# Scan sums from stacked high and low rows, transposes ahead of the state's products, and a later query transpose

## The chip, the cores and the metric

One core of a Trainium2 chip runs the whole program in one launch. The metric is the device time in microseconds (us); a profiled execution has a time of its own and a span, from its first to its last instruction. The kernel drives five instruction queues by hand: TensorE (PE: matmuls and transposes), VectorE (DVE), ScalarE (ACT), GpSimd (POOL) and SyncE (SP, which issues most DMAs). They meet only at semaphores.

## The reference, cut to what matters

Two layers. Each has three token mixers on one normalised input (a Mamba-2 scan, a gMLP, a dilated attention), an output projection and a gated FFN. The change touches the scan and the attention's queries. In the scan, for each chunk of 128 tokens, each of 2 directions and each of 8 heads (2 groups of 4), a 128x128 matrix of decays is needed:

```python
acs = jnp.cumsum((dt * a_neg).reshape(b, nc, q, g, hg), axis=2)
seg = acs[:, :, :, None] - acs[:, :, None, :]
decay_in = jnp.exp(jnp.where(tri[:, :, None, None], seg, NEG_INF))
cb = jnp.einsum('bctgn,bcsgn->bctsg', cc, bc)
y_diag = jnp.einsum('bctsg,bctsgh,bcsghp->bctghp', cb, decay_in, xdt)
states = jnp.einsum('bcsgn,bcsgh,bcsghp->bcghpn', bc, decay_out, xdt)
```

`y_off` adds what the state of the chunks before gives; the state goes from chunk to chunk in order.

## The kernel before, in words

All large products are float32 split in a high and a low part (fp32r), three matmuls per tile: weights high with input high, high with low, low with high. GpSimd makes the two parts of each weight unit (L475, L477) in two slots; PE frees a slot with its unit's first matmul of the next one (`w_used`).

**Layer, in the order of PE's queue.** Keys, queries, values (8 token tiles each), the 16 products `f` of the scan's input (`columns_tile`, 24 matmuls of 512 columns each, banks 0 and 1 in turn), attention with the gate's products between its steps, the backward states (`ra_`), the forward scan (`chunk`), the transposes of the mixers' outputs (`y_turn`), the output projection, the FFN.

**Keys and queries.** `heads_turn(f)`, f = 0 to 3, transposes 8 tiles of the normalised keys (f = 0, 1) or queries (2, 3) to PSUM banks 6 and 7. ACT takes the high part (`heads_high`, L1038) and DVE the low part (`heads_low`, L1446). `heads_turn(3)` waits until DVE has read banks 6 and 7 for f = 2, and that `heads_low(2)` waits for the copies KX<-KL by DMA (`keys_low`), since QL lies where KL lay. PE's queue has `heads_turn(3)` ahead of product f = 1. ACT's queue has `heads_high(3)`, two DMA issues (`queries_twice`), then `tap(0)` (it takes the products f = 0 and 1 from banks 0 and 1), `softplus`, `tap(1)` (products 2 and 3). Product f needs its bank emptied of product f - 2.

**Sums.** For chunk c, direction d and group g, bank 2 or 3 gets, for 4 heads, the sum of a mask (FAR: 0 or -1e30, by the identity IDR) and of the head's row of cumulated sums. Those rows lie transposed in the parameter tile `w_dt`, 128 rows: (chunk, direction, head). MH holds them in four copies, each with the rows of one head of the four and zeros elsewhere, ML the low parts. A stationary column of SEL, broadcast, picks the 4 rows of (c, d, g). So each of the four `sums` of a chunk is three matmuls of 512 columns: FAR, MH, ML (L803, L808). ACT takes the exponential (L1232).

**One chunk n in PE's queue** (`chunk`): the products of the states with C (L825, 8 instructions); sums j = 2 and 3; the gMLP's mix (L833) into bank 7; the state's products (L843) into the same bank 7, which first wait until DVE has read the mix (`gt_done`, GT, L1676); the next chunk's 6 transposes and 2 products B, C (`chunk_turn`, L792, L795); sums 0 and 1 of the next chunk; the 8 products within the chunk (L859), which wait for DVE's masked decays (`w_masked`, L1689).

**One chunk in DVE's queue** (L1669 to L1704): XW, CURF by its decay, Y1 from bank 5, GT from bank 7, Y3, YT's gMLP columns, twice the pair SEG add and SEG mask, CURF plus bank 7, Y1 three times, YT. **In ACT's:** XS from bank 0, BC from bank 1 (after the second mask), 8 exponentials, ST scaled, 8 more, Y2, the squares of the chunk before.

**Backward states** (`ra_`): PE's transposes (L743) and state products (L754); DVE XWA, BW; ACT BSTA, and at i = 2 IDR, SEL, MH; DVE at i = 4 `far` (FAR, ML). SP's queue reloads scan tiles (XBS, XBR) between two weight DMAs and the gates' loads.

Of the kernel before, what the change touches and what calls it, by code (L numbers as in the profile page):

```python
# [19 lines left out]
F32 = mybir.dt.float32  # L20
# [5 lines left out]
P = 128  # L26
# [107 lines left out]
def trunk(nc, xT, wst, params, consts, onehot, lnrow, table, outT):  # L134
# [10 lines left out]
    with ExitStack() as ctx:  # L145
# [12 lines left out]
        WH = place("WH", [P, W_AT[1] + 2048], dt=F32R)  # L158
        WL = place("WL", [P, W_AT[1] + 2048], dt=F32R)
        PARM = place("PARM", [P, NPAR])  # L160
        CST = place("CST", [P, 4 * P + 36])
        QSL = place("QSL", [P, AH_, P], top[0], F32R)
        U = place("U", [P, NT, 16])
        LDT = place("LDT", [P, NT, 16])
# [23 lines left out]
        NACS = place("NACS", [P, NT, 16])  # L188
        QGN = place("QGN", [P, 1])
        ident, tri_f, tri_b, ones = (CST[:, i * P:(i + 1) * P] for i in range(4))  # L190
        fourth, fours = CST[:, 4 * P:4 * P + 4], CST[:, 4 * P + 4:4 * P + 36]

        def par_(name, a=0, b=None):
            at, w = PAR[name]
# [70 lines left out]
        Y2 = work("Y2", [P, INNER])  # L265
        Y3 = work("Y3", [P, INNER])
        GT = work("GT", [P, GW])
        MH = place("MH", [P, 4, P], m_at[0], F32R)
        ML = place("ML", [P, 4, P], m_at[0] + 2048, F32R)
        IDR = place("IDR", [P, P], m_at[0] + 4096, F32R)  # L270
        FAR = place("FAR", [P, 2, P], m_at[0] + 4608, F32R)
        SEL = place("SEL", [P, 32], m_at[0] + 5632, F32R)
        assert m_at[0] + 5760 <= x_at

        PS = ctx.enter_context(nc.psum_tensor("PS", [P, 8, HALF], F32))

        def sem(name):
            return ctx.enter_context(nc.semaphore(name))
# [25 lines left out]
        xbs_used, zg_used = sem("xbs_used"), sem("zg_used")  # L304
        ra_t_full, ra_bst, ra_xw, ra_s_full, ra_done, ra_step = (
            sem("ra_t_full"), sem("ra_bst"), sem("ra_xw"), sem("ra_s_full"), sem("ra_done"), sem("ra_step"))
        acst_full, far_step = sem("acst_full"), sem("far_step")
        t_full, bst_ready, xs_ready = sem("t_full"), sem("bst_ready"), sem("xs_ready")
        ab_full, curf_ready, y12_done, gt_done = sem("ab_full"), sem("curf_ready"), sem("y12_done"), sem("gt_done")
        far_ready, ldt_ready = sem("far_ready"), sem("ldt_ready")  # L310
# [170 lines left out]
        def _(pe):  # L481
# [122 lines left out]
            for l in range(DEPTH):  # L604
# [47 lines left out]
                    pe.wait_ge(acs_ready, l + 1)  # L652
                    nc.tensor.transpose(PS[:, 4, 0:P], ACS[:].rearrange("p c e -> p (c e)"), ident).then_inc(acst_full, 1)

                between = {1: lambda: heads_turn(3), 6: decays, 8: decays_turn}
                for f in range(2 * XBC_T):
                    if f in between:
                        between[f]()
# [88 lines left out]
                def ra_state(i, par, first=False):  # L747
# [8 lines left out]
                                                XWA[:, par, g * 256:(g + 1) * 256], start=True, stop=True)  # L756
                    last.then_inc(ra_s_full, 1)

                def tile_in(i):
                    pe.wait_ge(xbs_full[i % 4], 16 * (l * (6 if i % 4 < 2 else 2) + i // 4 + 1))  # L760

# [8 lines left out]
                tile_in(1)  # L770
                ra_turn(1, 1)
                fold_head(STEPS - 1)
                ra_state(0, 0, first=True)
                pe.wait_ge(ra_t_full, l * NT + 2)
                pe.sem_inc(xbs_used, 1)
# [23 lines left out]
                def sums(n, j):  # L799

                        g, d = divmod(j, 2)
                        pe.wait_ge(exp_ready, n * 4 + j + 1)
                        nc.tensor.matmul(bank(2 + j % 2), IDR[:, :],  # L803
                                         FAR[:, d, :].unsqueeze(1).to_broadcast((P, 4, P)),
                                         start=True, stop=False, skip_group_check=True)
                        rows = n % NT * 4 + d * 2 + g
                        for part in (MH, ML):
                            last = nc.tensor.matmul(bank(2 + j % 2), SEL[:, rows:rows + 1].to_broadcast((P, P)),  # L808
                                                    part[:].rearrange("p h n -> p (h n)"), start=False,
                                                    stop=part is ML, skip_group_check=True)  # L810
                        last.then_inc(ab_full, 1)

                def chunk(i2, par, end):
                    c = i2 * 2 + par
                    n = l * NT + c

                    pe.wait_ge(curf_ready, 1 + n)
                    pe.wait_ge(y12_done, 1 + n)
                    if n:
                        pe.wait_ge(y2_ready, n)  # L820
                    for d in range(2):
                        for g in range(GROUPS):
                            cols = slice(g * 256, (g + 1) * 256)
                            st = CURF[:, cols] if d == 0 else BW[:, c + 1, cols]
                            last = nc.tensor.matmul(PS[:, 5 + d, cols], XBS[:, par, 6 + g, :], st,  # L825
                                                    start=True, stop=True)
                    last.then_inc(yo_full, 1)
                    sums(n, 2)
                    sums(n, 3)

                    pe.wait_ge(vn_ready, n + 1)
                    for g in range(GG):
                        last = nc.tensor.matmul(PS[:, 7, g * HD:(g + 1) * HD], par_("w_s", g * P, (g + 1) * P),  # L833
                                                ST[:, c // 4, c % 4, g * HD:(g + 1) * HD], start=True, stop=True)
                    last.then_inc(mx_full, 1)
                    pe.wait_ge(yo_full, n + 1)
                    pe.sem_inc(xbs_used, 1)

                    pe.wait_ge(bst_ready, n + 1)
                    pe.wait_ge(xw_ready, n + 1)  # L840
                    pe.wait_ge(gt_done, n + 1)
                    for g in range(GROUPS):
                        last = nc.tensor.matmul(PS[:, 7, g * 256:(g + 1) * 256], BC[:, 0, g, :],  # L843
                                                XW[:, g * 256:(g + 1) * 256], start=True, stop=True)
                    last.then_inc(sf_full, 1)
                    if not end:
                        pe.wait_ge(xbs_full[1 - par], 16 * (l * 6 + 2 + i2 + par + 1))
                        pe.wait_ge(bst_ready, n + 1)
                        chunk_turn(i2, 1 - par)
                        sums(n + 1, 0)  # L850
                        sums(n + 1, 1)

                    pe.wait_ge(xs_ready, n + 1)
                    pe.wait_ge(chunk_done, 1 + n)
                    for g in range(GROUPS):
                        pe.wait_ge(w_masked, 2 + n * 2 + g + 1)
                        for h in range(4):
                            e = g * 4 + h
                            last = nc.tensor.matmul(PS[:, 4, e * HD:(e + 1) * HD], SEG[par][:, 2 * g, h, :],  # L859
                                                    XS[:, par, e * HD:(e + 1) * HD], start=True, stop=True)  # L860
                    last.then_inc(yd_full, 1)
# [73 lines left out]
        def _(act):  # L935
# [85 lines left out]
            for l in range(DEPTH):  # L1021
# [84 lines left out]
                keys_low()  # L1106
                heads_high(2)
                act.wait_ge(row_out, 16)
                heads_high(3)
                queries_twice()  # L1110
                tap(0)
                softplus()
                tap(1)
                silu_out(0)
# [66 lines left out]
                for i in range(NT):  # L1181
                    n, par = l * NT + i, i % 2
                    act.wait_ge(ra_t_full, n + 1)
                    A(BSTA[:, par, :], PS[:, 1 + 3 * par, 0:GROUPS * STATE], ACT.Copy).then_inc(ra_bst, 1)
                    if i == 0:
                        gate(7)
                    if i == 2:
                        A(IDR[:], ident, ACT.Copy)
                        A(SEL[:], fours, ACT.Copy)
                        for h in range(4):  # L1190
                            last = A(MH[:, h, :], par_("w_dt"), ACT.Copy, scale=fourth[:, h:h + 1])
                        last.then_inc(far_step, 1)
                    if 1 <= i <= 4:
                        for t in range(2):
                            gate_square(2 * i - 2 + t)
                    if i == 6:
                        act.wait_ge(vinv_ready, l + 1)
                        A(VR[:], VSS[:], ACT.Sqrt).then_inc(vr_ready, 1)
# [19 lines left out]
                for c in range(NT):  # L1218
# [2 lines left out]
                    act.wait_ge(yz_ready, n + 1)  # L1221
                    A(XS[:, par], bank(0), ACT.Copy).then_inc(xs_ready, 1)
                    act.wait_ge(w_masked, 2 + n * 2)
                    A(BC[:].rearrange("p a g n -> p (a g n)"), bank(1), ACT.Copy).then_inc(bst_ready, 1)
                    for j in range(4):
                        g, d = divmod(j, 2)
# [74 lines left out]
        def _(dve):  # L1301
# [110 lines left out]
            for l in range(DEPTH):  # L1412
# [201 lines left out]
                def far():  # L1614
                    for d, tri in enumerate((tri_f, tri_b)):
                        TS(FAR[:, d, :], tri, 1.0, 1e30, ALU.subtract, ALU.mult)
                    dve.wait_ge(far_step, l + 1)
                    for h in range(4):
                        last = STT(ML[:, h, :], par_("w_dt"), fourth[:, h:h + 1], MH[:, h, :].bitcast(F32),
                                   ALU.mult, ALU.subtract)  # L1620
                    last.then_inc(far_ready, 1)

                step = Steps(dve, ra_step, 1)
# [218 lines left out]
def chip_constants():  # L1842
    i = np.arange(P)
    return np.concatenate([np.eye(P), i[:, None] <= i[None, :], i[:, None] >= i[None, :], np.ones((P, P)),
                           i[:, None] % 4 == np.arange(4), i[:, None] // 4 == np.arange(32)], axis=1).astype(np.float32)


def weight_stream(w_in, w_out, w_up, w_down):
# [73 lines left out]
```

## Time and profile before

| | |
|---|---|
| median of 3 runs | 2700.49 us (2696.34 to 2701.76) |
| profiled execution: time, span | 2702.63 us, 2700.8 us |
| busy: PE, DVE, ACT, POOL | 96%, 55%, 33%, 27% |
| mean granted TensorE clock | 0.986 |
| scan of layer 1, of layer 2 | some 436 to 520 us, 1764 to 1848 us |
| query stall of layer 1, of layer 2 | 123.5 to 129.2 us, 1452.0 to 1457.6 us |

Busy times of PE overlap by the end of one matmul and the start of the next; the distance from start to start is what a matmul costs in a full queue.

### The profile page before, as it was taken

How to read it: one execution, taken by the hardware profiler on the slowest of the kernel's cores; microseconds unless marked ns; L12 is line 12 of the kernel's file. 1: busy time of each engine (PE TensorE's matmuls, PEld its weight loads, DVE VectorE, ACT ScalarE, POOL GpSimd, SP SyncE). 2: the span in 40 equal slices, each digit the busy share in tenths (PEclk: the TensorE clock that was granted, in tenths of full speed). 3: DMA queues.
4: the chain of work that ended last, by engine and by line, in shares of the span. 5: the costliest groups of instructions: out<-in, count | busy, mean ns of one | idle time of the engine just before them, and what ended most of it. 6: DMA issues, size and time to landing. Idle time of an engine off the chain costs nothing.

```text
span 2700.8 us, 33553 instructions
## 1 busy us (share of the span) xinstructions
PE 2588.5 (96%) x13398; PEld 2188.8 (81%) x13398; DVE 1483.8 (55%) x1743; ACT 896.6 (33%) x1550; POOL 731.1 (27%) x388
## 2 busy tenths in 40 slices
PE   5999998899999999999999999898999999999998
PEld 5888987788888888888788889877878888888887
DVE  5466557837444444444564755686464444444455
ACT  3245556613222111111233465574131122211121
POOL 2332110023333333333323311200333333333331
PEclk9999999899999999999999999998999999999999
DMA  5434343121111111111122344521111111111111
GB/s 185 135 108 125 128 151 114 46 94 47 47 47 47 47 49 51 49 47 47 60 102 73 115 128 138 171 89 69 47 48 47 47 47 47 47 47 47 49 53 70
DMA packets 73724, 209.90 MB, mean 78 GB/s; under 512 B 5832, under 2 KB 28360, under 8 KB 72264
## 3 DMA queue, kind: packets, MB, share of 16 engines
q1 hardware_dynamic: 53384, 178.59, 20.0%
q10 hardware_dynamic: 20200, 29.30, 3.4%
q8 instruction: 106, 1.74, 0.3%
q14 instruction: 34, 0.28, 0.0%
HBM read 176.37 MB, written 31.49 MB: 77 GB/s over the span
## 4 chain that ended last, share of the span: by engine, by line
PE 87%; DVE 6%; ACT 3%; issue 2%; DMA 1%; POOL 0%; ACTq 0%; SPq 0%; DVEq 0%; POOLq 0%; PEldq 0%
PE PS L485 22%; PE PS L489 22%; PE PS L488 21%; PE PS L556 3%; PE PS L560 3%; PE PS L559 3%; PE PS L696 2%; PE PS L685 2%; DVE ACC L1311 1%; PE PS L808 1%; PE PS L825 1%; PE PS L859 1%; PE PS L675 1%; PE PS L674 1%; DVE CV L1484 1%
## 5 line engine op out<-in xcount | busy, mean ns | idle before, releaser
L485 PE MATMUL PS<-HH,WH 128*128 128x512 f32 x1920 | 760.2, 396 | 4.8 <-issue 4.8
L489 PE MATMUL PS<-HH,WL 128*128 128x512 f32 x1920 | 757.7, 395 | 0.0
L475 POOL CAST WH<-RAW 128x1024 fp32r<-128x1024 f32 x192 | 238.8, 1244 | 1910.7 <-PE PS L485 1430.3
L488 PE MATMUL PS<-HL,WH 128*128 128x512 f32 x1920 | 753.5, 392 | 0.0
L477 POOL TENSOR_TENSOR WL<-RAW,WH 128x1024 fp32r<-128x1024 f32 x192 | 498.0, 2594 | 15.4
L1740 DVE TENSOR_TENSOR X<-PS,X 128x512 f32<-128x512 f32 x384 | 259.3, 689 | 378.5 <-PE PS L489 378.0
L485 PEld LDWEIGHTS PS<-HH,WH 128*128 128x128 f32 x1920 | 363.0, 189 | 84.3 <-issue 5.6
L489 PEld LDWEIGHTS PS<-HH,WL 128*128 128x128 f32 x1920 | 362.4, 189 | 83.8
L488 PEld LDWEIGHTS PS<-HL,WH 128*128 128x128 f32 x1920 | 362.8, 189 | 82.1
L1270 ACT ACTIVATE FPAD<-PS 128x512 f32<-128x512 f32 x176 | 102.5, 596 | 890.5 <-PE PS L489 890.5
L1758 DVE SCALAR_TENSOR_TENSOR CVV<-FPAD,PARM,CVV 128x1024 f32<-128x1024 f32 x44 | 95.3, 2166 | 380.0 <-ACT CVV L1276 380.0
L485 PE MATMUL PS<-AHI,WH 128*128 128x512 f32 x704 | 277.4, 394 | 4.8 <-DVE X L1740 4.8
L489 PE MATMUL PS<-AHI,WL 128*128 128x512 f32 x704 | 278.5, 396 | 0.0
L488 PE MATMUL PS<-ALO,WH 128*128 128x512 f32 x704 | 276.5, 393 | 0.0
L556 PE MATMUL PS<-WH,HH 128*128 128x256 f32 (+1 forms) x896 | 262.1, 293 | 14.1 <-DVE HL L1332 14.1
L560 PE MATMUL PS<-WH,HL 128*128 128x256 f32 (+1 forms) x896 | 254.9, 284 | 0.0
L559 PE MATMUL PS<-WL,HH 128*128 128x256 f32 (+1 forms) x896 | 254.8, 284 | 0.0
L556 PEld LDWEIGHTS PS<-WH,HH 128*128 128x128 f32 x896 | 171.9, 192 | 17.1 <-DVE HL L1332 10.4
L560 PEld LDWEIGHTS PS<-WH,HL 128*128 128x128 f32 x896 | 172.4, 192 | 0.0
L559 PEld LDWEIGHTS PS<-WL,HH 128*128 128x128 f32 x896 | 171.7, 192 | 0.1
L485 PEld LDWEIGHTS PS<-AHI,WH 128*128 128x128 f32 x704 | 132.3, 188 | 36.5 <-DVE X L1740 6.6
L488 PEld LDWEIGHTS PS<-ALO,WH 128*128 128x128 f32 x704 | 132.3, 188 | 31.7
(198 smaller groups left out, 3122.6 us busy)
## 6 DMA issues: line engine op xcount, KB each, us to landing
RAW<-wst SPq DMA_DIRECT2D x192, 512.0 KB, 3.5
TOE<-toe_d SPq DMA_DIRECT2D x64, 512.0 KB, 3.7
XBS<-xbc_d SPq DMA_DIRECT2D x24, 512.0 KB, 4.4
xspill<-X ACTq DMA_DIRECT2D x2, 4096.0 KB, 12.3
xbc_d<-CV ACTq DMA_DIRECT2D x16, 512.0 KB, 4.5
X<-xspill SPq DMA_DIRECT2D x4, 2048.0 KB, 7.3
tok_d<-ST ACTq DMA_DIRECT2D x12, 512.0 KB, 3.4
ZG<-tok_d SPq DMA_DIRECT2D x16, 384.0 KB, 3.3
```

Source lines behind the costliest of these rows:

```text
L475: nc.gpsimd.tensor_copy(hi, raw).then_inc(hi_done, 1)
L477: nc.gpsimd.tensor_tensor(lo, raw, hi.bitcast(F32), ALU.subtract).then_inc(w_ready, 1)
L485: ins = nc.tensor.matmul(out, wh, xh, start=first, stop=False)
L488: nc.tensor.matmul(out, wh, xl, start=False, stop=False)
L489: return nc.tensor.matmul(out, wl, xh, start=False, stop=last)
L556: ins = nc.tensor.matmul(o, xh, wh, start=(k == 0), stop=False)
L559: nc.tensor.matmul(o, xh, wl, start=False, stop=False)
L560: return nc.tensor.matmul(o, xl, wh, start=False, stop=(k == KT - 1))
L685: last = nc.tensor.transpose(PS[:, 4 + t // 4, (t % 4) * P:(t % 4 + 1) * P], LG[:, j % 2, t * P:(t + 1) * P], ident)
L1270: A(FPAD[:, x % 2, 1 + th * HALF:1 + (th + 1) * HALF], bank(f % 4), ACT.Copy).then_inc(a_free, 1)
L1740: TT(x, bank(4 + i % 4), x, ALU.add).then_inc(b_free, 1)
L1758: step.then(STT(t, FPAD[:, x % 2, 0:SEQ], PARM[:, at:at + 1], t, ALU.mult, ALU.add))
```

## The change

- The 128 rows are cut into two parts of 64 (chunks 0 to 3, 4 to 7). `rows_twice` multiplies them with slices of the identity so that bank 6 holds, for each part, the same 64 rows twice, one above the other. MHL takes the place of MH and ML: partitions 0 to 63 hold the high rows and 64 to 127 the low rows. SEL has 16 columns that pick the 4 rows in both halves. A sum is two matmuls: FAR and MHL.
- `rows_twice` (4 products, fp32) stands in PE's queue ahead of the first backward state product. ACT's four copies and DVE's four subtractions read bank 6, two parts at once (256 columns; DVE on 64 partitions). ACT waits for `rows_full`.
- `chunk_turn` of the next chunk stands ahead of the state's products. ACT's copy to BC waits for the state's products of the chunk before (`sf_full`).
- `heads_turn(3)` stands ahead of product f = 2, not f = 1; ACT's `tap(0)` stands ahead of `heads_high(3)`.

```diff
-                between = {1: lambda: heads_turn(3), 6: decays, 8: decays_turn}
+                between = {2: lambda: heads_turn(3), 6: decays, 8: decays_turn}
...
+                def rows_twice():
+
+                    pe.wait_ge(ldt_ready, l + 1)
+                    for part in range(2):
+                        for low in range(2):
+                            last = nc.tensor.matmul(PS[low * 64:low * 64 + 64, 6, part * P:(part + 1) * P],
+                                                    ident[:, part * 64:part * 64 + 64], par_("w_dt"),
+                                                    start=True, stop=True, skip_group_check=True)
+                    last.then_inc(rows_full, 1)
...
                 fold_head(STEPS - 1)
+                rows_twice()
                 ra_state(0, 0, first=True)
...
-                        rows = n % NT * 4 + d * 2 + g
-                        for part in (MH, ML):
-                            last = nc.tensor.matmul(bank(2 + j % 2), SEL[:, rows:rows + 1].to_broadcast((P, P)),
-                                                    part[:].rearrange("p h n -> p (h n)"), start=False,
-                                                    stop=part is ML, skip_group_check=True)
-                        last.then_inc(ab_full, 1)
+                        part, c = divmod(n % NT, 4)
+                        rows = c * 4 + d * 2 + g
+                        nc.tensor.matmul(bank(2 + j % 2), SEL[:, rows:rows + 1].to_broadcast((P, P)),
+                                         MHL[:, part].rearrange("p h n -> p (h n)"), start=False, stop=True,
+                                         skip_group_check=True).then_inc(ab_full, 1)
...
+                    if not end:
+                        pe.wait_ge(xbs_full[1 - par], 16 * (l * 6 + 2 + i2 + par + 1))
+                        pe.wait_ge(bst_ready, n + 1)
+                        chunk_turn(i2, 1 - par)
                     pe.wait_ge(bst_ready, n + 1)
                     pe.wait_ge(xw_ready, n + 1)
                     pe.wait_ge(gt_done, n + 1)
...
-                        chunk_turn(i2, 1 - par)
                         sums(n + 1, 0)
                         sums(n + 1, 1)
...
+                tap(0)
                 heads_high(3)
                 queries_twice()
-                tap(0)
...
+                        act.wait_ge(rows_full, l + 1)
                         for h in range(4):
-                            last = A(MH[:, h, :], par_("w_dt"), ACT.Copy, scale=fourth[:, h:h + 1])
+                            last = A(MHL[:, :, h, :], PS[:, 6, 0:2 * P].rearrange("p (a n) -> p a n", a=2), ACT.Copy,
+                                     scale=fourth[:, h:h + 1])
...
                     act.wait_ge(w_masked, 2 + n * 2)
+                    if n:
+                        act.wait_ge(sf_full, n)
...
-                        last = STT(ML[:, h, :], par_("w_dt"), fourth[:, h:h + 1], MH[:, h, :].bitcast(F32),
-                                   ALU.mult, ALU.subtract)
+                        low = MHL[64:P, :, h, :]
+                        last = STT(low, PS[64:P, 6, 0:2 * P].rearrange("p (a n) -> p a n", a=2),
+                                   fourth[64:P, h:h + 1], low.bitcast(F32), ALU.mult, ALU.subtract)
```

## Rows read from the trace of the kernel before

**Rows 1.** The page's chain that ended last, by engine, whole span.
```profile
PE 87%; DVE 6%; ACT 3%; issue 2%; DMA 1%; POOL 0%; ACTq 0%; SPq 0%; DVEq 0%; POOLq 0%; PEldq 0%
```
**Rows 2.** Timeline, layer 1, PE: start us, us, instruction, idle before and its releaser.
```profile
114.09 1.03 PE L627 MATMUL PS<-CST,QN 128*128 128x128 f32 x8
...
123.26 0.39 PE L489 MATMUL PS<-HH,WL 128*128 128x512 f32 x1
...
129.16 1.94 PE L627 MATMUL PS<-CST,QN 128*128 128x128 f32 x8 [5.51 <-DVE QL L1446]
...
136.89 0.39 PE L485 MATMUL PS<-HH,WH 128*128 128x512 f32 x1
```
**Rows 3.** Timeline, layer 2, PE, the same place.
```profile
1457.62 1.94 PE L627 MATMUL PS<-CST,QN 128*128 128x128 f32 x8 [5.49 <-DVE QL L1446]
...
1466.61 0.39 PE L485 MATMUL PS<-HH,WH 128*128 128x512 f32 x1
```
**Rows 4.** Windows: us, busy of PE, PEld, DVE, ACT, POOL, clock, DMA share, GB/s.
```profile
129.20:132.00 2.80, 2.80 (x11) 2.61 (x12) 0.00 (x0) 0.80 (x1) 0.00 (x0) 0.51 0.00 0
```
**Rows 5.** Timeline, layer 2, ACT's queue: the second copy of the queries is issued.
```profile
1462.56 2.48 ACTq L1049 DMA_DIRECT2D QH<-QH  x1
```
**Rows 6.** Chain of waits in order of time, one chunk of layer 1.
```profile
453.45 0.44 DVE GT L1676
453.88 0.14 issue
454.02 1.10 PE PS L843 x4
455.12 0.66 PE PS L792 x6
455.78 0.45 PE PS L795 x4
...
456.45 0.48 PE PS L808 x2
...
457.62 1.73 PE PS L859 x16
459.35 1.78 PE PS L825 x8
...
462.53 0.85 PE PS L833 x8
```
**Rows 7.** Timeline, DVE, GT of the first chunk, and the way to the second's.
```profile
443.52 0.42 DVE L1676 TENSOR_TENSOR GT<-PS,PARM 128x256 f32<-128x256 f32 x1 [2.09 <-PE PS L833]
...
451.18 0.69 DVE L1669 TENSOR_TENSOR XW<-XS,WST 128x512 f32<-128x512 f32 x1
451.79 0.69 DVE L1672 TENSOR_TENSOR CURF<-CURF,CDEC 128x512 f32<-128x512 f32 x1
452.51 0.69 DVE L1674 TENSOR_TENSOR Y<-PS,EACS 128x512 f32<-128x512 f32 x1
453.45 0.42 DVE L1676 TENSOR_TENSOR GT<-PS,PARM 128x256 f32<-128x256 f32 x1 [0.25 <-PE PS L833]
```
**Rows 8.** Waits from 447 to 513 us: who for whom, us, times, longest.
```profile
DVE GT L1676 <- PE PS L833: 1.6, 6, 0.3
```
**Rows 9.** Windows, one chunk of the scan, and ten us of the backward states.
```profile
447.58:457.50 9.92, 9.31 (x60) 8.34 (x59) 9.29 (x16) 8.16 (x31) 0.00 (x0) 1.00 0.28 95
...
414.00:424.00 10.00, 7.53 (x43) 5.69 (x41) 9.83 (x16) 7.56 (x28) 2.71 (x2) 1.00 0.89 307
```
**Rows 10.** Timeline, backward states, all engines.
```profile
416.59 1.27 ACT L1191 ACTIVATE MH<-PARM,CST 128x128 fp32r<-128x128 f32 x4
...
418.76 1.10 PE L754 MATMUL PS<-XWA,BSTA 128*128 128x256 f32 x4 [1.55 <-DVE XWA L1594]
...
426.51 1.54 PE L743 MATMUL PS<-CST,XBR 128*128 128x128 f32 x6 [2.52 <-DMA XBR<-xbc_d]
...
1758.74 0.69 DVE L1635 TENSOR_TENSOR BW<-BW,PS 128x512 f32<-128x512 f32 x1 [0.78 <-PE PS L754]
```

More of the change, by code:

```diff
@@ L160, in trunk @@
         PARM = place("PARM", [P, NPAR])
-        CST = place("CST", [P, 4 * P + 36])
+        CST = place("CST", [P, 4 * P + 20])
         QSL = place("QSL", [P, AH_, P], top[0], F32R)
@@ L190, in trunk @@
         ident, tri_f, tri_b, ones = (CST[:, i * P:(i + 1) * P] for i in range(4))
-        fourth, fours = CST[:, 4 * P:4 * P + 4], CST[:, 4 * P + 4:4 * P + 36]
+        fourth, fours = CST[:, 4 * P:4 * P + 4], CST[:, 4 * P + 4:4 * P + 20]
         def par_(name, a=0, b=None):
@@ L267, in trunk @@
         GT = work("GT", [P, GW])
-        MH = place("MH", [P, 4, P], m_at[0], F32R)
-        ML = place("ML", [P, 4, P], m_at[0] + 2048, F32R)
+        MHL = place("MHL", [P, 2, 4, P], m_at[0], F32R)
         IDR = place("IDR", [P, P], m_at[0] + 4096, F32R)
         FAR = place("FAR", [P, 2, P], m_at[0] + 4608, F32R)
-        SEL = place("SEL", [P, 32], m_at[0] + 5632, F32R)
-        assert m_at[0] + 5760 <= x_at
+        SEL = place("SEL", [P, 16], m_at[0] + 5632, F32R)
+        assert m_at[0] + 5696 <= x_at
         PS = ctx.enter_context(nc.psum_tensor("PS", [P, 8, HALF], F32))
@@ L306, in trunk @@
             sem("ra_t_full"), sem("ra_bst"), sem("ra_xw"), sem("ra_s_full"), sem("ra_done"), sem("ra_step"))
-        acst_full, far_step = sem("acst_full"), sem("far_step")
+        acst_full, rows_full, far_step = sem("acst_full"), sem("rows_full"), sem("far_step")
         t_full, bst_ready, xs_ready = sem("t_full"), sem("bst_ready"), sem("xs_ready")
@@ L846, in chunk @@
                     if not end:
-                        pe.wait_ge(xbs_full[1 - par], 16 * (l * 6 + 2 + i2 + par + 1))
-                        pe.wait_ge(bst_ready, n + 1)
-                        chunk_turn(i2, 1 - par)
                         sums(n + 1, 0)
@@ L1844, in chip_constants @@
     return np.concatenate([np.eye(P), i[:, None] <= i[None, :], i[:, None] >= i[None, :], np.ones((P, P)),
-                           i[:, None] % 4 == np.arange(4), i[:, None] // 4 == np.arange(32)], axis=1).astype(np.float32)
+                           i[:, None] % 4 == np.arange(4), i[:, None] % 64 // 4 == np.arange(16)], axis=1).astype(np.float32)
 def weight_stream(w_in, w_out, w_up, w_down):
```

## The prediction
> **What bounds the kernel now.** I read the page first: the chain that ended last is PE for 87% [rows 1]. So the kernel is a full PE queue with holes, and the question for each edit is whether it removes PE time where PE sets the pace, or fills a hole. Two places are touched, and they turn out to be different.
>
> At the queries I read PE's timeline. After the last matmul of product f = 0 (start 123.26) PE does nothing until 129.16, when DVE has read the banks that the next 8 transposes write [rows 2]. Layer 2 has the same hole of 5.49 us [rows 3]. There is a second loss behind it: the 8 transposes take 1.94 us where the same 8 took 1.03 us at 114.09 [rows 2], and in the stretch from 129.2 to 132.0 the granted clock is 0.51, the 1.2 GHz level [rows 4]. PE had stood still 5.5 us before it fell.
>
> In the scan I read the chain in order of time, then DVE's timeline. The chain runs through PE alone but for one hole a chunk: GT 0.44 and issue 0.14, between the mix (L833) and the state's products (L843) [rows 6]. That looks like a PE bound. But DVE is busy 9.29 of 9.92 us in one chunk [rows 9], and of the rest it waits only 0.25 for PE, at GT, once a chunk [rows 7], 1.6 us in six chunks [rows 8]. What remains idle is DVE's own waits for its last result (451.79 to 452.51 is 0.72 where 451.18 to 451.79 is 0.61 [rows 7]). The scan is bound by both engines almost equally, and only PE is relieved.
>
> **The query transposes.** Removed: the hole. The new order puts the 24 matmuls of f = 1 into it. A 512-column matmul costs 0.23 us from start to start (a pair of L808 is 0.48, [rows 6], some 0.46 over many), so f = 1 takes 5.5 us: layer 1, 123.49 to 129.0. The transposes then start at 129.16 as before, since what releases them (DVE, behind the copy of the keys' low parts) does not move; nothing that DVE or that DMA waits for is touched. With PE never idle they run at the higher level: 1.03 less the 0.16 by which a record outlasts the distance to the next (0.39 against 0.23), 0.87 us. Product f = 2 starts at 130.03 in place of 136.89 [rows 2]: 6.86 us. Layer 2: 1457.62 + 0.87 = 1458.49 in place of 1466.61 [rows 3]: 8.12 us, more because more matmuls there ran at the lower level. Sum 14.98 us. Banks 0 and 1 are free for f = 0 and 1, the value tiles having left them before.
>
> What is late next? ACT now does `tap(0)` first. It copies bank 1 when f = 1 ends (129.2), 0.6 us, and a 1.25 us pass over the tile, so it reaches `heads_high(3)` at about 131.1, where before it was released at 131.2. The two DMA issues of `queries_twice` stand behind it, then `softplus`, some 3.6 us with its two table loads, then `tap(1)`, which frees bank 0 for f = 4. In layer 1 I get 139 us against f = 4 at 130.03 + 11.0 = 141.1: 2 us to spare. In layer 2 the second issue took 2.48 us [rows 5], and bank 0 is free at 1469.3 against 1469.5. That is the thinnest cover in this estimate. It costs nothing as it stands; if an issue takes that much longer again, 2 us. Everything after hangs on PE's products (the weights, conv passes, the decays before f = 6 and 8) and shifts with them.
>
> **The sums.** Four matmuls of 512 columns fewer in each chunk: 4 x 0.23 = 0.92 us of PE. **The order of transposes and state products.** They take 0.66 + 0.45 = 1.11 us [rows 6] and now lie in the hole of 0.44 + 0.14 + 0.02 = 0.60, which they cover. PE's need per chunk falls from 9.95 to 9.95 - 0.92 - 0.60 = 8.43 us.
>
> DVE's need is what counts then. The GT of the second chunk could start 0.61 after 452.51, at 453.12, and starts at 453.45 [rows 7]: 0.33 us. So DVE's period is 9.93 - 0.33 = 9.60 us, and 8.43 is below it. Is every release early enough? Counting from the end of the second mask (447.6, where the window of [rows 9] opens), PE has to do half of L859 (0.87), L825 (1.78), two sums (0.92), the mix (0.85) [rows 6]: 4.4 us; DVE reaches GT after 453.12 - 447.58 = 5.5 us. Room 1.1. ACT is busy 8.16 of 9.92 [rows 9] and waits now for PE's sums, which come earlier. Its new wait, for the state's products of the chunk before, ended some 2 us earlier than the second mask, which it waits for anyway; behind that copy stand the exponentials, so a late one would be dear, but it isn't late. The XBS tiles for the earlier transposes were loaded a chunk ahead.
>
> So each of the 7 steps from chunk to chunk gains 0.33 to 0.35 us, not 1.52: 2.4 us. In the first chunk DVE waits 2.09 us for the mix [rows 7], ahead of which stands one sum that starts when ACT's exponentials allow; it loses one matmul: 0.23. The tail after the last GT is DVE's and moves as a whole. 2.6 us a layer, 5.2 us in all. From below, the gain is 0 if another release takes GT's place; from above it is 1.52 x 16 = 24.3 if PE sets the pace.
>
> **What is added.** `rows_twice` is 4 fp32 products of 128 columns, 8 instructions, in the backward states. The trace has none of that shape; L795 (4 instructions in 0.45, [rows 6]) gives 0.11 each, 0.9 us, and by busy records of 0.27 each it would be 2.2. I take 0.9, the nearest in columns and kind. It stands ahead of the first state product; PE has 1.55 us of waiting for DVE shortly behind, and then 2.52 us for the DMA of XBR [rows 10], which is what this stage ends on. So 0; uncovered, +0.9 a layer. It also holds back the release of one XBS tile on SP's queue, with the weight and gate loads and XBR behind it; that queue then waits for GpSimd's half of a weight unit, which I count as cover, with the same 0.9 as the price. ACT's four copies (1.27 before) become 256 columns wide from PSUM: between nothing and double, I take +0.5; DVE needs them 9 us later. DVE's four subtractions grow likewise by about 0.5, and in layer 2 behind them DVE waits 0.78 for PE [rows 10]: 0, or 0.5 uncovered. SEL's smaller copy is nothing. A gain from these additions is excluded: nothing there gets shorter but SEL.
>
> **The sum.** From the profiled execution's own 2702.63 us (span 2700.8): - 15.0 - 5.2 = 2682.4. That execution is 2.1 us above the median of the runs shown, so 2680.5 as a median.
>
> **The rivals.**
> 1. *The clock falls inside the scan (slower).* PE will stand still some 1.2 us of 9.6 in each chunk, in three pieces, where now 0.6. If that makes the chip grant the 1.2 GHz level, PE's need grows. A matmul that costs 0.23 costs 0.43 there (8 transposes: 1.94 against 1.03, [rows 2]). It decides once PE's need passes 9.60, so when a sixth of its work is slow; with half of the work slow the need is 8.43 x 1.43 = 12.1 us, 2.1 over now, and 14 steps give +30: 2702.6 - 15 + 30 = 2717. Against it: from 414 to 424 us PE is busy only 7.53 of 10, with a hole of 1.55, and the clock stays 1.00 [rows 9, 10]. The Trainium skill's page "TensorE: Matmul & The Clock Gate", section "A second HAM failure mode: psum-queue depth-cycling", says that PE pausing briefly and often between groups of matmuls can make the clock oscillate; by that rule this rival would be the likely case. The rows of 414 to 424 speak against it here, and I keep it at 0.06.
> 2. *PE alone sets the pace in the scan.* All 24.3 us come through: 2702.6 - 15 - 24.3 = 2663. For it: the chain names PE everywhere in the scan. Against it: DVE's 9.29 busy of 9.92, in which I find no time to give. 0.05.
> 3. *ACT's queue takes over at the queries.* Bank 0 for f = 4, or the queries' high parts, come late by some 2 us a layer: 2686.5. For it, the 0.2 us of cover in layer 2. 0.08.
> 4. *The scan gives nothing,* because GT finds another wait (the exponentials behind which the second pair of sums stands) or the additions come uncovered: 2687.6 to 2690. 0.07.
>
> **How the numbers follow.** Forecast 0.74, rivals 0.06, 0.05, 0.08, 0.07. Rivals 3 and 4 lie within 2692, to which the range goes; below it goes to 2673 for a scan that gives more than DVE's sum says and for the spread of the runs. Rivals 1 and 2 are left out. A measurement of this kernel tells a change of about 0.2% (5.4 us) from none. Faster 0.93; within it 0.03; slower 0.04 (rival 1 in full).
>
> **What would show it.** Queries: no wait of PE for DVE QL at L627 in either layer, the transposes in 1.0 us, clock 1.00 after them, f = 2's first matmul 0.9 us behind their start. Scan: period of 9.6 us, DVE waiting for PE at GT no more, PE waiting about 1.2 us a chunk at L843 (for GT) and L859 (for the mask). Additions: `rows_twice` in about 1 us, and the wait for XBR still there. I am wrong if the period is below 9.5 (DVE was not the bound), if the clock in the scan's window is under 1.00, or if a wait of PE for ACT's PAD copies appears at f = 4.

## The result, and the profile after

The kernel after takes 2678.0 us (median of 6 runs, 2674.9 to 2681.2), the kernel before beside it 2700.2 us (6 runs, 2696.3 to 2701.8): ratio 0.992, interval 0.9907 to 0.9933, or 22.2 us less. Forecast were 2680.5 us and a range of 2673 to 2692.

The profiled execution of after took 2681.2 us (span 2679.4), 21.4 us less than that of before. Cut into stages at instructions that both kernels have (the backward states begin at the memset of BW):

| Stage, profiled executions | before, us | after, us | difference | forecast |
|---|---|---|---|---|
| start to the first key transposes, layer 1 | 91.17 | 94.45 | +3.28 | 0 |
| from there to the backward states, layer 1 | 321.97 | 314.95 | -7.02 | -6.86 |
| the same, layer 2 | 323.19 | 314.92 | -8.27 | -8.12 |
| backward states to the first GT, layer 1 | 30.38 | 28.10 | -2.28 | -0.23 |
| the same, layer 2 | 28.76 | 28.09 | -0.67 | -0.23 |
| first to last GT (7 steps), layer 1 | 69.60 | 67.11 | -2.49 | -2.4 |
| the same, layer 2 | 69.59 | 67.11 | -2.48 | -2.4 |
| last GT of layer 1 to key transposes of layer 2 | 906.53 | 908.18 | +1.65 | 0 |
| last GT of layer 2 to the end | 859.61 | 856.49 | -3.12 | 0 |

The places of the change give 20.3 us at the queries and in the scan's steps. The other 1.1 us is the balance of three places that gain and two that lose (the backward states gain 2.95 us, of which 0.46 was forecast). The +3.28 lies ahead of every edited line: in all the traces of this study, of whichever kernel, those transposes start between 86.6 and 94.5 us.

**The queries.** PE's timeline in the kernel after, layer 1, around the transposes of the last query head (start us, us, instruction; a wait would stand in brackets):

```profile
131.96 0.39 PE L488 MATMUL PS<-HH,WL 128*128 128x512 f32 x1
132.38 1.06 PE L626 MATMUL PS<-CST,QN 128*128 128x128 f32 x8
133.20 0.48 PE L484 MATMUL PS<-HH,WH 128*128 128x512 f32 x1
...
1450.29 0.39 PE L488 MATMUL PS<-HH,WL 128*128 128x512 f32 x1
1450.66 1.06 PE L626 MATMUL PS<-CST,QN 128*128 128x128 f32 x8
1451.48 0.49 PE L484 MATMUL PS<-HH,WH 128*128 128x512 f32 x1
```

The last matmul of f = 1 starts 0.42 us ahead of the transposes (0.37 in layer 2) and no wait is left, where [rows 2, 3] have 5.51 and 5.49 us. The transposes take 1.06 us instead of 1.94, and the first matmul of f = 2 starts 0.82 us behind their start. Counted from the key transposes, the query transposes start where they did (37.93 us against 37.99), so all that is gained lies behind them.

ACT in layer 2 of the kernel after, the engine with the thin cover:

```profile
1452.50 2.23 ACT L1048 ACTIVATE QH<-PS,QGN 64x1024 fp32r<-64x1024 f32 x2
...
1455.40 0.62 ACTq L1059 DMA_DIRECT2D QH<-QH  x1
...
1459.76 0.60 ACT L1083 ACTIVATE PAD<-PS 128x512 f32<-128x512 f32 x1
```

The second issue of the queries' copy, 2.48 us in [rows 5], takes 0.62 here. Bank 0 is read at 1459.8 to 1460.4 and f = 4 wants it at about 1451.5 + 11.0 = 1462.5: 2 us to spare. PE waits for ACT nowhere in this stage.

**The scan.** DVE's timeline in the kernel after, GT of the first chunk, then the way to two later ones:

```profile
437.50 0.42 DVE L1691 TENSOR_TENSOR GT<-PS,PARM 128x256 f32<-128x256 f32 x1 [2.31 <-PE PS L842]
...
445.16 0.69 DVE L1684 TENSOR_TENSOR XW<-XS,WST 128x512 f32<-128x512 f32 x1
445.77 0.68 DVE L1687 TENSOR_TENSOR CURF<-CURF,CDEC 128x512 f32<-128x512 f32 x1
446.49 0.69 DVE L1689 TENSOR_TENSOR Y<-PS,EACS 128x512 f32<-128x512 f32 x1
447.10 0.41 DVE L1691 TENSOR_TENSOR GT<-PS,PARM 128x256 f32<-128x256 f32 x1
...
456.68 0.41 DVE L1691 TENSOR_TENSOR GT<-PS,PARM 128x256 f32<-128x256 f32 x1
```

GT now starts 0.61 us behind Y, with nothing in brackets; [rows 7] has 0.94 us, of which 0.25 was a wait. The period is 9.58 to 9.60 us in all 14 steps of the two layers (9.93 to 9.95 before). PE's timeline of a chunk after shows the other side:

```profile
446.19 0.82 PE L802 MATMUL PS<-CST,XBS 128*128 128x128 f32 x6
446.85 0.61 PE L805 MATMUL PS<-XBS 128*128 128x128 f32 x4
447.65 1.10 PE L856 MATMUL PS<-XW,BC 128*128 128x256 f32 x4 [0.19 <-DVE GT L1691]
...
450.04 1.08 PE L869 MATMUL PS<-XS,SEG 128*128 128x64 f32 x8 [0.36 <-DVE SEG L1704]
...
451.28 1.10 PE L869 MATMUL PS<-XS,SEG 128*128 128x64 f32 x8 [0.16 <-DVE SEG L1704]
```

The transposes of the next chunk (L802, L805) stand where PE stood still, and the brackets of PE's waits come to 0.71 us a chunk, all of it for DVE. A bracket counts from the end of the last record, which outlasts the distance to the next matmul by some 0.16 us. From start to start PE loses some 0.35 us ahead of L856 (0.80 from L805, whose 4 instructions take 0.45 in [rows 6]), and 0.53 and 0.33 us ahead of the two halves of L869: 1.2 us in all. The waits of the kernel after from 438 to 504 us (who for whom, us, times, longest):

```profile
PE PS L869 <- DVE SEG L1704: 3.3, 13, 0.4
...
PE PS L856 <- DVE GT L1691: 1.2, 6, 0.2
...
ACT SEG L1246 <- PE PS L818: 2.4, 7, 0.4
```

The row of [rows 8] is gone: DVE waits for PE's mix no more, and PE waits for DVE. Windows of the kernel after (us, busy of PE, PEld, DVE, ACT, POOL, clock, DMA share, GB/s): queries, backward states, one period of the scan.

```profile
118.00:135.00 17.00, 16.96 (x92) 14.46 (x91) 3.62 (x10) 5.80 (x7) 6.84 (x4) 1.00 0.47 124
412.40:437.50 25.10, 17.54 (x94) 13.31 (x95) 21.25 (x35) 14.11 (x44) 0.66 (x1) 1.00 0.47 169
441.56:451.14 9.58, 8.87 (x54) 7.59 (x54) 9.19 (x16) 8.16 (x31) 0.00 (x0) 1.00 0.29 98
```

The clock is 1.00 in all three; in [rows 4] it is 0.51 behind the query hole.

**The additions.** Timeline of the kernel after, backward states of layer 1:

```profile
409.77 0.66 PE L763 MATMUL PS<-PARM,CST 128*64 128x128 f32 x8
410.36 1.13 PE L753 MATMUL PS<-XWA,BSTA 128*128 128x256 f32 x4
...
412.84 1.56 ACT L1202 ACTIVATE MHL<-PS,CST 128x256 fp32r<-128x256 f32 x4
...
421.53 0.88 PE L742 MATMUL PS<-CST,XBR 128*128 128x128 f32 x6 [1.26 <-DMA XBR<-xbc_d]
422.31 1.70 DVE L1634 SCALAR_TENSOR_TENSOR MHL<-PS,CST,MHL 64x256 fp32r<-64x256 f32 x4
...
424.84 1.10 PE L753 MATMUL PS<-XWA,BSTA 128*128 128x256 f32 x4 [0.37 <-DVE XWA L1608]
```

The 8 instructions of `rows_twice` take 0.59 us from start to start, ACT's copies 1.56 us against 1.27 [rows 10], and the wait for XBR is still there.

### The profile page after: what moved, and what is told of

Its sections match the earlier page's. It is cut to its first block and busy times, and to the rows that moved or that the text cites. A ratio compares the mean times of both kernels' runs of the same rounds, so it can differ in the third digit from the quotient of the medians.

```text
span 2679.4 us, 33472 instructions
## 1 busy us (share of the span) xinstructions
PE 2575.6 (96%) x13350; PEld 2177.3 (81%) x13350; DVE 1482.6 (55%) x1743; ACT 896.7 (33%) x1550; POOL 730.8 (27%) x388
## 3 DMA queue, kind: packets, MB, share of 16 engines
q1 hardware_dynamic: 53384, 178.58, 20.3%
## 5 line engine op out<-in xcount | busy, mean ns | idle before, releaser
L488 PEld LDWEIGHTS PS<-AHI,WL 128*128 128x128 f32 x704 | 132.9, 189 | 31.3
## 6 DMA issues: line engine op xcount, KB each, us to landing
xspill<-X ACTq DMA_DIRECT2D x2, 4096.0 KB, 13.1
```

The costliest lines, as they stand in the source:

```text
L488: return nc.tensor.matmul(out, wl, xh, start=False, stop=last)
```

## The experiments

Each kernel was timed in the same rounds as the kernel before on the same chip. Below, "step" is the distance from one GT (or what stands in its place) to the next.

**The query part alone.** The kernel before with two edits:

```
-                between = {1: lambda: heads_turn(3), 6: decays, 8: decays_turn}
+                between = {2: lambda: heads_turn(3), 6: decays, 8: decays_turn}
...
+                tap(0)
                 heads_high(3)
-                tap(0)
```

> The kernel before with the query part alone: heads_turn(3) ahead of product f = 2 and ACT's tap(0) ahead of heads_high(3). My theory (two separate terms, 15.0 for the queries and 5.2 for the scan): 15 us faster than before, some 2685; the profile has no wait of PE for DVE QL, the scan keeps its period of 9.93 us, and the clock still falls in the backward states behind the wait for XBR. Rival (the whole of the 22 us measured comes from here, since the clock stays up longer after the hole is gone): 20 us or more faster. Rival (ACT's queue takes over): 11 us or less.

Measured: 2684.8 us (6 runs), ratio 0.9944 (0.993 to 0.9958), 15.5 us less. From the key transposes to the backward states it takes 315.12 us in layer 1, after 314.95. Its steps stay at 9.92 to 9.95 us, and DVE still waits for the mix in each. DVE's timeline of this kernel:

```profile
431.30 0.42 DVE L1676 TENSOR_TENSOR GT<-PS,PARM 128x256 f32<-128x256 f32 x1 [2.08 <-PE PS L833]
...
441.22 0.42 DVE L1676 TENSOR_TENSOR GT<-PS,PARM 128x256 f32<-128x256 f32 x1 [0.23 <-PE PS L833]
```

So this part is worth what the forecast said (14.98), and the scan's steps don't depend on it.

**The order alone.** The kernel before, with the next chunk's transposes ahead of the state's products and the wait on ACT that this needs:

```
             (PE, behind the mix)
+            if not end:
+                ...
+                chunk_turn(i2, 1 - par)
             ... the state's products ...
-            if not end:
-                ...
-                chunk_turn(i2, 1 - par)
             (ACT, ahead of the copies of the transposes)
+            if n:
+                act.wait_ge(sf_full, n)
```

> The kernel before with the order in the scan alone: the next chunk's transposes ahead of the state's products, with ACT's new wait. Theory (DVE sets the pace once PE is relieved at all): PE's need falls to 9.95 - 0.60 = 9.35 us a chunk, still under DVE's 9.60, so the period is 9.58 to 9.60, as in the whole change, and the kernel is 4.9 us faster. Rival (PE alone sets the pace, each edit gives its own part): period 9.35, 14 x 0.60 = 8.4 us or more faster. The query hole stays.

Measured: 2695.5 us (12 runs), ratio 0.9989 (0.998 to 0.9998), 4.8 us less. DVE's timeline: a step of 9.59, no wait.

```profile
449.67 0.41 DVE L1679 TENSOR_TENSOR GT<-PS,PARM 128x256 f32<-128x256 f32 x1
...
459.26 0.41 DVE L1679 TENSOR_TENSOR GT<-PS,PARM 128x256 f32<-128x256 f32 x1
```

**The stacked sums alone.** The kernel before with `rows_twice`, `MHL` and one product for each sum; both order edits left as they were:

```
-                for part in (MH, ML):
-                    last = nc.tensor.matmul(bank(2 + j % 2), SEL[:, rows:rows + 1].to_broadcast((P, P)), part ...)
+                nc.tensor.matmul(bank(2 + j % 2), SEL[:, rows:rows + 1].to_broadcast((P, P)), MHL[:, part] ...)
```

> The changed kernel with the query part and the order part undone: only the stacked sums, with rows_twice. Theory: PE's need falls to 9.95 - 0.92 = 9.03 us, under DVE's 9.60, so the period is again 9.58 to 9.60 and the gain 5.2 us, the same as for the order alone, and both together give no more than one. Rival (PE sets the pace): period 9.03, 14.7 us faster. It also has rows_twice without the query part: if the backward states end earlier because rows_twice keeps PE busier, their clock stays at 1.00 here and falls in the two kernels without it; from the second state product's start to the first GT the stage would be some 2 us shorter in layer 1.

Measured: 2694.5 us (12 runs), ratio 0.9978 (0.9969 to 0.9986), 5.8 us less. The steps are 9.58 to 9.60 us here too, but for the first of layer 1. Windows of this kernel, that step and the one behind it:

```profile
441.85:453.64 11.79, 11.17 (x54) 9.83 (x54) 9.20 (x15) 7.14 (x28) 0.00 (x0) 0.73 0.17 61
453.64:463.23 9.59, 8.42 (x54) 7.60 (x54) 9.20 (x16) 8.69 (x35) 0.00 (x0) 1.00 0.29 94
```

In the first of them the clock stood at its lower level for 6.3 us, PE needed more than DVE, and the step was 2.2 us longer; in the second it is back at 1.00. That is what rival 1 said a lower clock would cost, for one step of 14, but not the cause that it named: by the trace's clock record the clock fell at 441.36 us, 0.5 us ahead of the first GT, before the scan's steps had begun.

The expectation's other guess, that `rows_twice` keeps the clock up in the backward states, failed. This kernel has `rows_twice`, and from the backward states to the first GT it took 30.25 and 28.56 us at a mean clock of 0.88 and 0.94, as long as the kernels without it.

The steps of the three runs read together: either scan edit alone takes 0.34 us off each, and both together take off 0.34, not 0.68. By PE's need they free different amounts (0.60 and 0.92 us). What they meet is one and the same floor.

**A DVE instruction less, in both kernels.** If DVE is that floor, an instruction less on it changes nothing before and everything after. The Y3 addition goes from each chunk, in the kernel before and in the kernel after:

```
-                step = Steps(dve, chunk_step, 6)
+                step = Steps(dve, chunk_step, 5)
...
-                step.then(TT(Y1[:], Y1[:], Y3[:], ALU.add))
```

> The kernel before with one DVE instruction less in each chunk: the addition of Y3 (the skip term, x by d_skip) to Y1 is left out, so the skip term is missing from the scan's output. It takes 0.72 us of DVE from start to start and nothing waits for it elsewhere. Theory (before, PE with its hole needs 9.95 us a chunk and DVE 9.60): the period stays 9.93 to 9.95, the same time within 0.05%, but for up to 0.7 us at each layer's tail. Rival (DVE already sets the pace before): period 9.2 to 9.3, 10 us faster.

> The changed kernel with the same instruction left out (the addition of Y3 to Y1, so the skip term is missing from the output). Theory (after the change DVE sets the pace and PE needs 8.43): period 9.59 - 0.72 = 8.87 us, 14 x 0.72 = 10 us plus up to 1.4 at the two tails faster than the changed kernel, some 2667. Rival (the scan is held by PE or ACT at 9.58): the same period.

> The changed kernel itself, to have it on the same chip and in the same rounds as the three beside it, and to see what differs between two of its executions: all of my theories give 2678 within 0.1%, the scan's period 9.58 to 9.60 in both layers, no wait at the query transposes. What may differ by the run is where the lower clock falls outside the scan (backward states, output transposes).

Measured in the same rounds: before without it 2699.0 us (11 runs), ratio 0.9993 (0.9984 to 1.0002), no change that can be told. Its timeline (DVE) shows a step of 9.94, and the wait at GT, 0.25 before, has grown to 0.34. Most of the freed time goes into a new wait of 0.7 us in each chunk, for PE's products within the chunk; the last line is from the waits of 455 to 495 us:

```profile
452.97 0.42 DVE L1676 TENSOR_TENSOR GT<-PS,PARM 128x256 f32<-128x256 f32 x1 [0.34 <-PE PS L833]
...
462.91 0.42 DVE L1676 TENSOR_TENSOR GT<-PS,PARM 128x256 f32<-128x256 f32 x1 [0.35 <-PE PS L833]
...
DVE Y L1701 <- PE PS L859: 2.7, 4, 0.7
```

After without it: 2670.6 us (4 runs), 5.6 us under the kernel after of the same rounds (2676.2, 5 runs). Its step, in DVE's timeline, is 8.89:

```profile
444.41 0.41 DVE L1691 TENSOR_TENSOR GT<-PS,PARM 128x256 f32<-128x256 f32 x1
...
453.30 0.41 DVE L1691 TENSOR_TENSOR GT<-PS,PARM 128x256 f32<-128x256 f32 x1
```

That is 0.70 us a step, what one such instruction costs (0.61 from start to start, 0.72 where it needs the result before it [rows 7]). The pair settles which engine sets the pace: PE before, DVE after. The time did miss the 10 to 11.4 us that I expected. Between first and last GT this trace gains 4.1 us in layer 1 (the first step there took 9.62, the clock having fallen 0.6 us ahead of the first GT) and 4.85 in layer 2, 9 in all. The rest went back outside the scan, where this execution has more of the lower clock: 75.6 us in its whole span, against 52.8 in that of the kernel after.

**`rows_twice` four times over.** The kernel after with

```
-                    for part in range(2):
+                    for part in (0, 1) * 4:
```

> The changed kernel with rows_twice done four times over (16 products in place of 4, the same result). One set took 0.59 us of PE from start to start, so 1.8 us more a layer. Theory (PE has waits in the backward states that cover it: for DVE 0.8 us, for the DMA of XBR 1.3 us and more): no slower than the changed kernel beyond 0.5 us. Rival (uncovered): 3.5 us slower. If filling PE there keeps its clock up, the stage does not get longer and its granted clock stays 1.00.

Measured: 2674.2 us (4 runs), ratio to before 0.9904 (0.9889 to 0.9919), not above the kernel after of the same rounds (2676.2). PE's timeline of this kernel:

```profile
403.74 1.97 PE L763 MATMUL PS<-PARM,CST 128*64 128x128 f32 x32
405.64 0.70 PE L753 MATMUL PS<-XWA,BSTA 128*128 128x256 f32 x2
```

Four sets take 1.90 us, 0.06 an instruction, and from the backward states to the first GT it takes 28.08 and 28.23 us as in after (28.10, 28.09). One set, 0.59 us, is hidden with room. The first step of layer 2 took 9.72 us here, again with a lower clock that began ahead of the first GT (1745.93 and 1746.37 us).

**The bias as a product, to go on from there.** DVE being the floor, work of it should go to PE, which has room. The gMLP bias is added by one more product of the mix, identity times the broadcast bias, and DVE multiplies the bank straight into YT:

```
-                    ... start=True, stop=True)
-                last.then_inc(mx_full, 1)
+                    ... start=g == 0, stop=False, ...)
+                nc.tensor.matmul(PS[:, 7, 0:GW], ident, par_("b_s").unsqueeze(2).to_broadcast((P, GG, HD)),
+                                 start=False, stop=True, ...).then_inc(mx_full, 1)
...
-                TT(GT[:] ..., PS[:, 7, 0:GW] ..., per_head(par_("b_s")), ALU.add ...)
-                TT(YT[:, c, INNER:INNER + GW], GT[:], ZG[:, par, 2, :], ALU.mult)
+                TT(YT[:, c, INNER:INNER + GW], PS[:, 7, 0:GW], ZG[:, par, 2, :], ALU.mult ...)
```

> The changed kernel, and one DVE instruction less in each chunk: the gMLP bias is added by PE (one more fp32 product of 256 columns, identity by the broadcast bias, into bank 7), and DVE multiplies bank 7 by the gate at once, where it had GT and then YT. Theory (DVE sets the pace): the period falls by the distance of one 256-column instruction, 0.34 us, and by the wait between the two, some 0.35 to 0.7 in all, to between 8.9 and 9.25; PE's need rises by 0.45 to 8.88, still below. 16 x 0.35 to 0.7 = 5.6 to 11 us faster than the changed kernel, 2667 to 2673. Rival (PE or ACT sets the pace in the changed kernel): no faster, or 7 us slower by PE's added product.

> The changed kernel with the gMLP bias added by PE, once more, now beside the changed kernel on the same chip. Its scan was 2.35 us shorter in each layer, its median in other rounds only 2 us and less below. Theory (the scan's gain is real, and what differs is where the lower clock falls outside it): period 9.25, median 3 to 5 us below the changed kernel of these rounds. Rival (a shorter scan is given back in the stages behind it in every execution): no difference in the median.

Measured: 2675.9 us (5 runs), ratio 0.9909 (0.9895 to 0.9924), and once more 2674.7 (5 runs), 0.9911 (0.9898 to 0.9925). The step is 9.24 to 9.26 us in both, at the weak end of what was expected (8.9 to 9.25), and the time misses the expected 2667 to 2673. One part of the gain is given back: from the transposes of the first chunk (PE, XBS) to the first GT, or the YT in its place, it takes 8.23 us instead of 7.75, as the mix that DVE waits for there ends later by the added product. That is 1.0 us over both layers. The step, in DVE's timeline of the first:

```profile
442.67 0.42 DVE L1694 TENSOR_TENSOR YT<-PS,ZG 128x256 f32<-128x256 f32 x1
...
451.93 0.41 DVE L1694 TENSOR_TENSOR YT<-PS,ZG 128x256 f32<-128x256 f32 x1
```

**And a wait moved.** DVE's wait for the output tiles, which stood between two instructions at the end of a chunk, goes behind the next chunk's XW:

```
+                if c:
+                    dve.wait_ge(yz_ready, 2 + n)
+                    dve.sem_inc(zg_used, 1)
...
-                dve.wait_ge(yz_ready, 2 + n + 1)
-                dve.sem_inc(zg_used, 1)
...
+                (behind the last chunk)
+                dve.wait_ge(yz_ready, 2 + (l + 1) * NT)
+                dve.sem_inc(zg_used, 1)
```

> The kernel with the bias on PE, and DVE's wait for its own last product of the chunk (for the release of the gate tile, 0.84 us from YT to XW where 0.61 is the distance without a wait) moved behind the next chunk's XW. Theory (DVE sets the pace, at 9.25 us, PE needs 8.88): the period falls by 0.23 to 9.02 us, 3.2 us less in the two scans than with the bias alone. Rival (PE or ACT takes over just below 9.25): the period stays at 9.2 or more.

> The changed kernel, as the partner of the two others in the same rounds: 2676 to 2678, period 9.59.

Measured: 2673.2 us (5 runs), ratio 0.9908 (0.9895 to 0.9922), with the kernel after at 2677.5 (5 runs, 0.9917) in the same rounds. The step is 9.02 to 9.05 (expected 9.02), by DVE's timeline of this kernel:

```profile
442.25 0.42 DVE L1697 TENSOR_TENSOR YT<-PS,ZG 128x256 f32<-128x256 f32 x1
...
451.28 0.42 DVE L1697 TENSOR_TENSOR YT<-PS,ZG 128x256 f32<-128x256 f32 x1
```

Over both scans the bias as a product takes 67.11 x 2 - 64.73 x 2 = 4.8 us off, and the moved wait brings it to 7.7. The medians of the same rounds move by 2.7 us (expected 3 to 5) and 4.3 us. The intervals overlap: this is the fastest version that I ran by median and by its steps, and by time alone it is not told apart from the kernel after.

## Why the prediction was right

**The query hole** (forecast 6.86 and 8.12, measured 7.02 and 8.27, alone 15.5 for both). Each step held: f = 1 fills the hole, the transposes cost 0.82 instead of 0.87, and the loss of the lower clock goes with the hole. That second loss had to be counted apart, and it explains why layer 2 gives more: the lower clock lasted 6.8 us there (1456.3 to 1463.1) and 3.4 us in layer 1 (128.5 to 131.9). These times are from the trace's clock record. By it the clock fell while PE still stood, 1.3 and 0.7 us before the transposes began, and not behind the hole as the prediction reads it. ACT's order was changed together with PE's, and no run tells the two apart.

**The scan's steps** (forecast 0.33 to 0.35 us each and a period of 9.60, measured 0.34 to 0.36 and 9.58 to 9.60). The step that carried it was to set PE's own need (9.95 falling to 8.43) against DVE's (9.60). The runs show it three ways: the wait for the mix is gone from DVE's rows, two unlike reliefs of PE give the same and don't add, and DVE's instruction is worth nothing before and 0.70 after. Rival 2 (PE alone, 2663) is refuted: with its 1.52 us off each step the period would have been 8.4.

**PE's waits** were put at 1.2 us a chunk. The brackets show 0.71, but the forecast counted from start to start, and counted so they are 1.2 as well. PE's need is 9.58 less 1.2, or 8.4 us, against the forecast's 8.43.

**The first chunk and the backward states** (forecast 0.23 a layer, measured 2.28 and 0.67). Here the forecast was too small, but its own term came as forecast: from the transposes of the first chunk (XBS) to the first GT it is 7.98 us in both layers before and 7.75 after, 0.23 less. The rest, 2.05 and 0.44 us, lies ahead of that and goes with the clock: in all eleven stages at the full clock, in kernels with the whole change, those transposes start 20.3 us behind the memset, whether XBR's wait ended 12.1 or 13.1 us behind it. From just before ACT's copy to IDR, up to GT, the granted clock was 0.88 in the kernel before and 1.00 in the kernel after, with the same work between. Windows of the kernel before, and under it of the kernel after without the Y3 addition:

```profile
416.14:443.52 27.38, 19.88 (x94) 15.07 (x93) 20.73 (x35) 14.13 (x45) 0.65 (x1) 0.88 0.43 155
```
```profile
407.75:434.79 27.04, 20.24 (x94) 15.59 (x95) 21.38 (x36) 14.39 (x45) 0.65 (x1) 0.86 0.43 155
```

The second has all of the change and the low clock all the same. Three executions of the kernel after itself took 28.10, 28.24 and 30.36 us in layer 1. So it differs from execution to execution. But chance alone is not shown either: in the five traces of kernels that lack a part of the change, the clock falls at or just behind the wait for XBR in both layers, ten times of ten; in the eight with all of it, five times of sixteen, and in layer 2 the three of after agree (28.08 to 28.09 us at 1.00). What decides it stays open.

**The additions** were costed at nothing. For `rows_twice` the run with four sets shows it. The sizes: `rows_twice` 0.59 where I took 0.9 (I priced it by products with a full 128-column stationary tile; this one has 64), ACT's copies +0.29 where I took 0.5, DVE's subtractions 1.70 against the 1.13 that four took before, +0.57 where I took 0.5. The last is not wholly covered in layer 1: PE waits 0.37 us behind them for XWA. Whether the 0.57 costs time stays open: no trace of a kernel with the old subtractions has this stage at the full clock.

**Rival 1 (the clock falls in the scan)** had the cost right, where a lower clock meets the scan, and the cause is not seen. In 4 of the 13 traces the lower clock reaches into the first step of one scan: the stacked sums alone (11.79 us), after without Y3 (9.62 against 8.9), four sets of `rows_twice` (9.72), and the third trace of the kernel after, whose step is 9.59 all the same. Windows of that step:

```profile
433.57:443.16 9.59, 9.59 (x57) 8.85 (x56) 9.20 (x16) 7.17 (x27) 0.00 (x0) 0.87 0.21 71
```

PE is busy throughout, and DVE still sets the pace. In all four the clock fell 0.4 to 0.9 us ahead of the first GT, at the end of the backward states. Between the first and the last GT it fell in none of the 13 traces. In the kernel after PE pauses three times in a chunk and is granted 1.00 behind the first step. The rule that I had weighed for it, in the Trainium skill's page "TensorE: Matmul & The Clock Gate", section "A second HAM failure mode: psum-queue depth-cycling", tells of a kernel whose frequent short pauses made the clock swing; in this scan they did not.

**Rival 3 (ACT's queue)** did not come: the DMA issue that took 2.48 us took 0.62, and the cover was 2 us instead of 0.2. It is no fixed property of layer 2: of the four traces with the old order of the queries it took 2.48 and 2.34 us in two and 0.63 in the others, and 0.62 in all nine with the new one. What sets it is not shown. **Rival 4** fell with the steps.

**Outside the change**, +3.28, +1.65 and -3.12 us nearly cancel. The last goes in part with a stretch at the lower clock behind the scan of layer 2: 20.5 us of it in the traces of before and of the three parts run alone, 10.2, 10.2 and 13.6 in the three of after. But the clock is not all of it. With the same 20.5 us this last stage takes 859.2 to 859.7 us in the four kernels with the old sums, and some 858 us in the stacked sums alone and in after without Y3. I didn't expect it, and didn't find what sets it. In sum the change was put at 20.2 us and came as 22.2 by the medians, 21.4 in the profiled pair, 20.3 of it in the terms that carried the forecast. (2682.4 less 2.1 is 2680.3, not the 2680.5 that the prediction names.)

## What to carry to other kernels

When the chain of waits runs through one engine with only small holes, add up what each of the two busiest engines needs for one period: the gain of relieving the first ends where the second's need begins, and edits that relieve the same engine then don't add. Test it with a pair, the same instruction taken from the second engine in the old and in the new kernel. And price a hole with what runs at the lower clock behind it, which here was 1.5 us (7.02 gained less the hole of 5.51) to 2.8 us (8.27 less 5.49) on top of the hole.

## What the runs showed of the hardware

The time that one execution spends at the lower TensorE clock varies between executions of the same kernel: 62.9, 52.8 and 66.5 us of the span in three traces of after, 55.4 and 69.0 in two of the version with the bias as a product, and 41.7 to 83.1 over all 13 traces. It comes in stretches, most of them at the same few places (the start, the backward states, the output behind a scan), each there or not. A gain of 4.8, 7.7 and 9.0 us in the scan's steps came out as 2.7, 4.3 and 5.6 in the medians. For the first two, which have the bias as a product, 1.0 us of the difference is the cost ahead of the first chunk; for the rest I can't say whether it is this, or a real cost elsewhere.

Fp32 products with a 64-column stationary tile cost 0.06 to 0.07 us for 128 columns an instruction (0.59 for 8, 1.90 for 32), less than the 0.11 of those with 128 (0.45 for 4, [rows 6]).
